# Attention scores: bias and maximum in one VectorE instruction, one score matmul, and the head split moved to ScalarE and GpSimd

## The reference, cut to what matters

```python
s_loc = jnp.einsum('bjqhd,bkjchd->bhjqkc', qb, k_slab, preferred_element_type=F32) * NA_SCALE
s_loc = jnp.where(mask6, s_loc + bias[None], -jnp.inf)
s_ctx = jnp.einsum('bjqhd,bmhd->bhjqm', qb, kc, preferred_element_type=F32) * NA_SCALE
s = jnp.concatenate([s_loc.reshape(B, H, n_cb, NB_COLS, n_loc), s_ctx], axis=-1)
p = jax.nn.softmax(s, axis=-1).astype(v.dtype)
o = (jnp.einsum('bhjqkc,bkjchd->bjqhd', p_loc, v_slab)
     + jnp.einsum('bhjqm,bmhd->bjqhd', p[..., n_loc:], vc))
```

## Time and profile before

| | us |
|---|---|
| median of 3 runs | 2961.95 |
| lowest and highest of the runs | 2944.74 and 2966.42 |
| the profiled execution's own time | 2960.28 |
| its span | 2958.5 |
| TensorE busy | 2811.8 (95%) |
| VectorE, ScalarE, GpSimd busy | 1488.5, 767.6, 884.8 |
| mean granted TensorE clock | 0.961 of full |

### The profile page before, as it was taken

One profiled execution on the slowest core, in us unless ns is written; L12 is line 12 of the kernel. 1 busy time (PEld: TensorE's weight loads), 2 busy tenths in 40 slices (PEclk: granted clock), 3 DMA queues, 4 the chain that ended last, 5 costly groups with the idle time before them and its releaser, 6 DMA issues.

```text
span 2958.5 us, 40428 instructions
## 1 busy us (share of the span) xinstructions
PE 2811.8 (95%) x15289; PEld 2625.9 (89%) x15289; DVE 1488.5 (50%) x2513; ACT 767.6 (26%) x1035; POOL 884.8 (30%) x355
## 2 busy tenths in 40 slices
PE   6899999999999989999999999999998887899998
PEld 6799999998965889999999899999997775778887
DVE  6666455655324265554665622422327888432233
ACT  1322111112134232211112322111114666332222
POOL 0232223322311122232333222322323443344442
PEclk6899999999969999999999999999999998999999
DMA  5244334432300023433444122312211111233332
GB/s 194 85 113 122 99 113 122 134 85 75 107 5 19 27 77 110 130 108 111 118 116 117 51 64 83 102 56 64 74 54 44 53 53 50 65 96 100 89 104 80
DMA packets 413083, 256.78 MB, mean 87 GB/s; under 512 B 6653, under 2 KB 405846, under 8 KB 413014
## 3 DMA queue, kind: packets, MB, share of 16 engines
q1 hardware_dynamic: 413014, 255.87, 29.9%
HBM read 252.70 MB, written 4.25 MB: 87 GB/s over the span
## 4 chain that ended last, share of the span: by engine, by line
PE 64%; issue 20%; DVE 7%; POOL 5%; ACT 3%; DMA 0%; SPq 0%; POOLq 0%; DVEq 0%; ACTq 0%
PE pair_b L1536 28%; PE pair_a L1536 27%; POOL w_lo L641 5%; PE pair_c L1586 2%; DVE decay L1496 1%; PE pair_c L1817 1%; DVE ada_sums L1015 1%; DVE decay L1494 1%; DVE h_lo L1154 1%; PE pair_b L1792 1%; DVE gate_i L1490 1%; PE pair_a L1776 1%; PE pair_a L1777 1%; PE pair_a L1778 1%; PE pair_a L1526 1%
## 5 line engine op out<-in xcount | busy, mean ns | idle before, releaser
L641 POOL TENSOR_TENSOR w_lo<-raw,w_hi 128x1024 fp32r<-128x1024 f32 (+3 forms) x302 | 825.4, 2734 | 1843.7 <-ACT w_hi L733 1843.7
L733 ACT ACTIVATE w_hi<-raw 128x1024 fp32r<-128x1024 f32 (+3 forms) x302 | 337.2, 1117 | 1284.9 <-PE pair_b L1536 438.8
L1045 DVE TENSOR_TENSOR work_g<-work_s,pair_b 128x768 f32<-128x768 f32 (+1 forms) x88 | 78.1, 888 | 698.7 <-PE pair_b L1536 535.9
L1015 DVE SCALAR_TENSOR_TENSOR ada_sums<-ada_raw,cvec,ada_sums 128x256 f32<-128x256 f32 x896 | 395.6, 514 | 0.0
L1536 PE MATMUL pair_a<-h_hi,w_hi 128*128 128x384 f32 x1312 | 340.7, 340 | 12.6 <-POOL w_lo L641 9.6
L1536 PE MATMUL pair_a<-h_lo,w_hi 128*128 128x384 f32 x1312 | 335.7, 337 | 0.0
L1536 PE MATMUL pair_a<-h_hi,w_lo 128*128 128x384 f32 x1312 | 335.6, 337 | 0.0
L1536 PE MATMUL pair_b<-h_hi,w_hi 128*128 128x384 f32 x1168 | 296.9, 335 | 3.8 <-POOL w_lo L641 3.8
L1536 PE MATMUL pair_b<-h_hi,w_lo 128*128 128x384 f32 x1168 | 296.7, 334 | 0.0
L1536 PE MATMUL pair_b<-h_lo,w_hi 128*128 128x384 f32 x1168 | 296.6, 334 | 0.0
L1536 PEld LDWEIGHTS pair_a<-h_hi,w_hi 128*128 128x128 f32 x1312 | 236.2, 190 | 16.7 <-issue 12.6
(11 more groups left out here) (273 smaller groups left out, 4602.6 us busy)
## 6 DMA issues: line engine op xcount, KB each, us to landing
raw<-in_ffn_w_gu_dram SPq DMA_DIRECT2D x176, 512.0 KB, 4.0
ada_raw<-in_ada_w_dram SPq DMA_DIRECT2D x64, 1024.0 KB, 5.2
raw<-in_ffn_w_down_dram SPq DMA_DIRECT2D x64, 704.0 KB, 5.3
raw<-in_rg_w_in_dram SPq DMA_DIRECT2D x20, 512.0 KB, 3.8
ada_first<-in_ada_w_dram SPq DMA_DIRECT2D x4, 2048.0 KB, 17.6
raw<-in_ab_w_in_dram SPq DMA_DIRECT2D x16, 512.0 KB, 3.9
raw<-in_rg_w_out_dram SPq DMA_DIRECT2D x8, 640.0 KB, 4.4
raw<-in_ab_w_out_dram SPq DMA_DIRECT2D x8, 512.0 KB, 4.1
```

The source lines that it names most:

```text
L641: nc.gpsimd.tensor_tensor(wl[:, par, 0:kt * P], raw[:, par, 0:kt * P], wh[:, par, 0:kt * P].bitcast(F32), ALU.subtract).then_inc(split_rea ...
L733: nc.scalar.activation(wh[:, par, 0:kt * P], raw[:, par, 0:kt * P], ACT.Copy).then_inc(hi_done, 1)
L1015: step = nc.vector.scalar_tensor_tensor(out=sums[v], in0=tiles(k), scalar=c_k, in1=sums[v], op0=ALU.mult, op1=ALU.add)
L1045: nc.vector.tensor_tensor(gbuf[:, 0, 0:W], sbuf[:, 0, 0:W], up, ALU.mult)\
```

## The change

It computes the same result with the work laid out in another way.

- Queries are scaled by a negative factor, and mask and bias are built with opposite sign, so that the scores in PSUM are negated. A latent step's scores are one product of 512 columns, whose keys are two runs of 256 columns in `k_t`. The product of identity and bias is gone.
- One DVE instruction, `tensor_tensor_reduce`, reads the 512 negated scores from PSUM and the bias (a run of 256 columns of bias, then 256 zeros) from SBUF, writes their sum to `prob` in SBUF and the minimum of each row to `neg_max`. It takes the place of `reduce_max`.
- ACT's exponential reads `prob` in SBUF, in place, with scale -1. `prob` has three buffers, the row statistics four.
- `scores(s)` waits for the new DVE instruction of `s - 2` and no longer for the exponential. The wait for a head's bias moves from PE to DVE, POOL's wait for a free bias buffer moves from the score matmul to the new DVE instruction.
- `take_heads` on DVE keeps the two copies. The high part is made by ACT (`heads_high`, at `j` = 5 of heads 2, 4, 6, and after the loop) and the low part by POOL (`heads_low`, after the bias of heads 3, 5, 7, and after the loop).
- PE starts the output projection when the four pooling tiles are split, and waits for each head tile where it is first read. `values` of a new pair of heads waits for the copies alone.
- `prob` moves to the place of `p_t`, `prob_t` and the bias table to other free places.

```diff
+            def heads_low(t):
+
+                pool.wait_ge(heads_hi, t + 1)
+                nc.gpsimd.tensor_tensor(hl[:, KP + t, :], att_f[:, t % 2, :], hh[:, KP + t, :].bitcast(F32),
+                                        ALU.subtract).then_inc(mixed_split, 1)
...
-                    pool.wait_ge(scores_done, (BLOCKS + 2) * (h - 2) + BLOCKS)
+                    pool.wait_ge(max_done, (BLOCKS + 2) * (h - 2) + BLOCKS)
                 for v in range(3):
                     t = bass.AP(tensor=table[:, :, :].tensor, offset=table[:, h % 2, SHIFT[v]:SHIFT[v] + 1].offset,
                                 ap=[list(table[:, 0, 0:1].ap[0]), [1, SLAB], [RPB_C, GRID_R]])
-                    last = nc.gpsimd.tensor_tensor(bias[:, h % 2, v, :].rearrange("p (c r) -> p c r", r=GRID_R), t,
-                                                   mask[:, v, :].rearrange("p (c r) -> p c r", r=GRID_R), ALU.add)
+                    last = nc.gpsimd.tensor_tensor(bias[:, h % 2 * 3 + v, :].rearrange("p (c r) -> p c r", r=GRID_R),
+                                                   mask[:, v, :].rearrange("p (c r) -> p c r", r=GRID_R), t, ALU.subtract)
                 last.then_inc(bias_done, 1)
+                if h in (3, 5, 7):
+                    heads_low(h // 2 - 1)
+            heads_low(KP - 1)
...
+            def heads_high(t):
+
+                act.wait_ge(heads_taken, t + 1)
+                nc.scalar.activation(hh[:, KP + t, :], att_f[:, t % 2, :], ACT.Copy).then_inc(heads_hi, 1)
+
             for s, (h, j) in enumerate(STEPS):
                 W = NK + CTX if j < BLOCKS else CTX
-                b = s % 2
 
                 act.wait_ge(max_done, s + 1)
-                if s >= 2:
-                    act.wait_ge(turned_done, s - 1)
-                nc.scalar.activation(prob[:, b, 0:W], pA[:, b * 512:b * 512 + W], ACT.Exp, bias=rowmax[:, b:b + 1],
-                                     accum_out=rowsum[:, b:b + 1]).then_inc(prob_done, 1)
+                nc.scalar.activation(prob[:, s % 3, 0:W], prob[:, s % 3, 0:W], ACT.Exp, bias=rowmax[:, s % 4:s % 4 + 1],
+                                     scale=-1.0, accum_out=rowsum[:, s % 4:s % 4 + 1]).then_inc(prob_done, 1)
                 if s >= 1:
                     copy_turned(s - 1)
+                if j == 5 and h % 2 == 0 and h >= 2:
+                    heads_high(h // 2 - 1)
             copy_turned(len(STEPS) - 1)
+            heads_high(KP - 1)
...
-                    dst, scale = (kT, 1.0) if n == 2 else (qT, DH ** -0.5)
+                    dst, scale = (kT, 1.0) if n == 2 else (qT, -DH ** -0.5)
...
-            def normalise(s):
+            def lowest(s):
+
                 h, j = STEPS[s]
                 W = NK + CTX if j < BLOCKS else CTX
                 b = s % 2
+                if j == 0:
+                    dve.wait_ge(bias_done, h + 1)
+                if s >= 3:
+
+                    dve.wait_ge(turned_done, s - 2)
+                add = bias[:, 6, :]
+                if j < BLOCKS:
+
+                    n = h % 2 * 3 + VARIANT[j]
+                    add = bass.AP(tensor=bias[:, :, :].tensor, offset=bias[:, n, 0:1].offset,
+                                  ap=[list(bias[:, 0, 0:1].ap[0]), [(6 - n) * NK, 2], [1, NK]])
+                src, to = pA[:, b * 512:b * 512 + W], prob[:, s % 3, 0:W]
+                if j < BLOCKS:
+                    src, to = [a.rearrange("p (g n) -> p g n", n=NK) for a in (src, to)]
+                dve.wait_ge(scores_done, s + 1)
+                nc.vector.tensor_tensor_reduce(out=to, in0=src, in1=add, scale=1.0, scalar=3.0e38, op0=ALU.add, op1=ALU.min,
+                                               accum_out=rowmax[:, s % 4:s % 4 + 1]).then_inc(max_done, 1)
+
+            def normalise(s):
+
+                j = STEPS[s][1]
+                W = NK + CTX if j < BLOCKS else CTX
                 dve.wait_ge(prob_done, s + 1)
-                chain(nc.vector.reciprocal(rowinv[:, b:b + 1], rowsum[:, b:b + 1]))
-                nc.vector.tensor_scalar(prob[:, b, 0:W], prob[:, b, 0:W], rowinv[:, b:b + 1], None, ALU.mult)\
-                    .then_inc(prob_scaled, 1)
+                nc.vector.reciprocal(rowinv[:, s % 4:s % 4 + 1], rowsum[:, s % 4:s % 4 + 1]).then_inc(inv_done, 1)
+                dve.wait_ge(inv_done, s + 1)
+                nc.vector.tensor_scalar(prob[:, s % 3, 0:W], prob[:, s % 3, 0:W], rowinv[:, s % 4:s % 4 + 1], None, ALU.mult)                    .then_inc(prob_scaled, 1)
 
             def take_heads(t):
 
                 dve.wait_ge(pv_done, (2 * t + 2) * (BLOCKS + 2))
+
+                dve.wait_ge(mixed_split, KP + t - 1)
                 f = att_f[:, t % 2, :]
                 o, oc = pC[:, (t % 2) * 512:(t % 2) * 512 + SEQ], pR[:, (t % 2) * 512:(t % 2) * 512 + CTX]
                 nc.vector.tensor_copy(f[:, 0:SEQ].rearrange("p (r c) -> p r c", c=GRID_W),
                                       o[:, ::-1].rearrange("p (c r) -> p r c", r=GRID_R))
-                chain(nc.vector.tensor_copy(f[:, SEQ:T], oc))
-                chain(nc.vector.tensor_copy(hh[:, KP + t, :], f))
-                nc.vector.tensor_tensor(hl[:, KP + t, :], f, hh[:, KP + t, :].bitcast(F32), ALU.subtract)\
-                    .then_inc(mixed_split, 1)
+                nc.vector.tensor_copy(f[:, SEQ:T], oc).then_inc(heads_taken, 1)
 
             for s, (h, j) in enumerate(STEPS):
-                W = NK + CTX if j < BLOCKS else CTX
-                b = s % 2
-
-                dve.wait_ge(scores_done, s + 1)
-                nc.vector.reduce_max(rowmax[:, b:b + 1], pA[:, b * 512:b * 512 + W], AX_X, negate=True)\
-                    .then_inc(max_done, 1)
+                lowest(s)
                 if s >= 1:
                     normalise(s - 1)
                 if j == 3 and h % 2 == 0 and h >= 2:
                     take_heads(h // 2 - 1)
             normalise(len(STEPS) - 1)
-            take_heads(3)
+            take_heads(KP - 1)
...
-                    pe.wait_ge(prob_done, s - 1)
+                    pe.wait_ge(max_done, s - 1)
                 else:
                     pe.wait_ge(proj_done, 2 + 16)
                 bank = pA[:, b * 512:(b + 1) * 512]
                 if j < BLOCKS:
                     q = qT[rows, t, (BLOCKS - 1 - j) * P:(BLOCKS - j) * P]
-                    if j == 0:
-                        pe.wait_ge(bias_done, h + 1)
                     k0 = SLAB_AT[j] * GRID_R
-                    nc.tensor.matmul(bank[:, 0:NK], q, kT[rows, t, k0:k0 + NK], start=True, stop=False)
-                    nc.tensor.matmul(bank[:, 0:NK], ident[:, :], bias[:, h % 2, VARIANT[j], :], start=False, stop=True)
-                    last = nc.tensor.matmul(bank[:, NK:NK + CTX], q, kT[rows, t, SEQ:T], start=True, stop=True)
+                    keys = bass.AP(tensor=kT[:, :, :].tensor, offset=kT[rows, t, k0:k0 + 1].offset,
+                                   ap=[list(kT[rows, t, 0:1].ap[0]), [SEQ - k0, 2], [1, NK]])
+                    last = nc.tensor.matmul(bank[:, :].rearrange("p (g n) -> p g n", n=NK), q, keys, start=True, stop=True)
...
-                    pe.wait_ge(mixed_split, KP + t - 1)
+                    pe.wait_ge(heads_taken, t - 1)
...
-            pe.wait_ge(mixed_split, 2 * KP)
-            outputs("about", P_ABOUT, KD, hh, hl)
+            pe.wait_ge(mixed_split, KP)
+            outputs("about", P_ABOUT, KD, hh, hl, 0, lambda k: k >= KP and pe.wait_ge(mixed_split, k + 1))
```

More of the change, by code:

```diff
@@ L228, in trunk @@
         kT = att("k_t", [P, KP, T])
+        pool_at = g_at + 2 * size([P, T // P, KP * P]) + size([P, SLABS, KP * P]) + size([P, KP, T])
         pT = att("p_t", [P, KP, PADW])
+        assert pool_at == g_at + size([P, T // P, KP * P]) + size([P, SLABS, KP * P]) + 2 * size([P, KP, T])
+        late = alias(pool_at, g_end)
+        prob = late("prob", [P, 3, 512])
         att_f = at("mixed", [P, 2, T], F32, g_at)
@@ L232, in trunk @@
         v_rows = gbuf[:, 1, :]
-        prob = at("prob", [P, 2, 512], F32, scr_at)
-        prob_t = at("prob_t", [P, 2, 512], F32, scr_at + size([P, 2, 512]))
+        prob_t = at("prob_t", [P, 2, 512], F32, scr_at)
         att2 = alias(scr_at + size([P, 4, T]), SBUF_END)
-        bias = att2("bias", [P, 2, 3, NK])
-        table = att2("rpb_table", [P, 2, TABLE])
+        bias = att2("bias", [P, 2 * 3 + 1, NK])
+        table = at("rpb_table", [P, 2, TABLE], F32, scr_at + size([P, 2, PADW]))
         mask = att2("mask", [P, 3, NK])
-        rowmax = att2("neg_max", [P, 2])
-        rowsum = att2("row_sum", [P, 2])
-        rowinv = att2("row_inv", [P, 2])
+        rowmax = att2("neg_max", [P, 4])
+        rowsum = att2("row_sum", [P, 4])
+        rowinv = att2("row_inv", [P, 4])
         inv_n = att2("inv_n", [P, NB])
@@ L337, in trunk @@
         prob_done = sem("prob_done")
+        inv_done = sem("inv_done")
         prob_scaled = sem("prob_scaled")
+        heads_taken = sem("heads_taken")
+        heads_hi = sem("heads_hi")
         turned_done = sem("turned_done")
```

(11 more changed lines are left out.)

## The result

The changed kernel takes 2910.44 us (median of 4 runs, 2909.76 to 2915.29), the kernel before 2954.39 (median of 4, 2944.74 to 2966.42) beside it. The ratio is 0.9853, with a 95% interval of 0.9807 to 0.9898: 1.0 to 1.9% faster. The forecast was 2926, with a range of 2898 to 2948. The profiled execution took 2915.29 us, 45.0 less than that of before.

A forecast was written before the change was run, and what follows sets the result against it. TensorE was taken to bound the attention. Gains of 25.3 (score products), 0.7 (start), 2.1 (head split), 3.0 (hole) and 3.0 (half clock behind it) sum to 34.1 us, from 2960.3 to 2926 us, range 2898 to 2948.

The forecast's parts named there:

- Products: Attention: one score product of 512 columns at 1.04 us replaces three totalling 1.89, per latent step at 2.4 GHz.
- Start, waits and hole: TensorE gains 0.7 us at the third score, 2.1 at three head-split waits, 3.0 ahead of the output projection.
- The half clock behind the hole: Output projection's first 5.94 us at half clock should go with the hole before it: 3.0 us gained.
- I take the same time, 51.1 us: Attention's start: the low clock stretch keeps its length in time, so 4.0 us of the gain are given back.
- the early clock rival: Attention's start: about 5 us at half clock in place of 51, 21 us more off, 2905 us; chance 0.17.
- the low stretch's length is far from 51 us: Sign at the attention's start by which the forecast is wrong; about 51 us at half clock was expected.
- POOL beside DVE: Head split's low part on POOL: runs beside DVE's scaling of `prob` without delay, cost nothing in the sum.
- No wait of TensorE for DVE in the loop: Expected sign in the profile after: TensorE never waits for DVE in the attention loop.
- The cover of the loop: Loop through DVE and ACT: TensorE has 3.8 us of other work against some 3.2 needed, so cost 0.
- The bound at which DVE itself would limit the loop: Attention loop: DVE becomes the bound only if its new instruction takes above 1.9 us per latent step.
- The end: Output projection starts at once, removing TensorE's 2.96 us standstill: 3.0 us gained; last head tile ready in time.
- The weights' overhead: Score products keep 0.18 us per change of stationary operand, so the wide one costs 1.04 us and not 0.86.

The follow-up runs named there:

- experiment 9: Changed kernel with three score products of 256 columns in place of the one of 512: 2932.06 us (11 runs), ratio 0.9932 to the kernel before.
- experiment 1: Changed kernel with the head split back on DVE and TensorE waiting for all eight head tiles: 2925.16 us (10 runs), ratio 0.9932 to before.
- experiment 2: Kernel before with only the head split moved to ACT and POOL and TensorE's late waits: 2939.6 us (10 runs), ratio 0.999.
- experiment 5: Changed kernel with TensorE waiting for all eight head tiles before the output projection: 2915.72 us (4 runs), ratio 0.9876 to before.
- experiment 6: Changed kernel with the new DVE instruction issued twice for each step: 2925.29 us (8 runs), ratio 0.9911 to before.
- experiment 7: Changed kernel with the heads' low part made by DVE in place of POOL: 2912.92 us (4 runs), ratio 0.9867 to before.
- experiment 8: Changed kernel run again, unaltered: 2912.99 us (4 runs), ratio 0.9866 to before.
- experiment 4: Changed kernel with idle products in TensorE's gap at the start, three behind the second score product, one behind the third: 2907.91 us (4 runs), ratio 0.9869.
- experiment 11: Changed kernel with idle products in TensorE's gap at the start, repeated with more runs: 2906.41 us (5 runs), ratio 0.9839 to before.
- experiment 3: Kernel before with two idle products in TensorE's gap ahead of the third score product: 2938.09 us (10 runs), ratio 0.9975.
- experiment 10: Changed kernel with the split on DVE, waiting for all eight tiles, idle products in all TensorE gaps: 2917.57 us (5 runs), ratio 0.9876.

## Why the prediction was right and where it was not

**The sum for TensorE held.** The four stretches without half clock put it together: 149.25 (before, filled), 142.86 (three narrow products), 126.81 (split on DVE, filled), 119.78 (changed, filled). The prediction's terms at full clock are 30 latent steps of 0.85, 0.7, 2.1 and 3.0, together 31.3; 149.25 - 119.78 = 29.5 was measured, or 30.0 without the 0.4 and 0.9 us that the idle products cost. Products 24.0 against 25.5: the steps inside the heads gave 0.825 each (17.09 - 13.79 for four), two waits of TensorE for the scaling, 0.2 us each, are new, and of the third step's 0.85 only 0.3 came off, because its transposes wait for the softmax's start (11.49 us behind the first pooling product, against 11.80 in experiment 9). Start, waits and hole together 6.0 (149.25 - 0.4 - 142.86) against 5.8; the start alone gave 0.8 (10.73 - 9.92) against 0.7. The half clock behind the hole, 3.0 us, is gone.

**The step that failed is "I take the same time, 51.1 us".** The low stretch at the start was 10.2 us in the profile after, and 10.2 to 13.7 in experiments 1, 2, 5, 6, 7 and 8. The 40.9 us less at half clock are 18.4 us, and 2926 - 18.4 = 2907.6 is what the early clock rival said (2905, with 5 us). That rival, at 0.17, described the profile better than the forecast did: the measured 2910 lies outside the 2918 to 2934 that had 0.50, and "the low stretch's length is far from 51 us" was one of the two signs by which the forecast was to be wrong. The wide range, 2898 to 2948, holds the result because it took the rival in. The profile of before was an execution of its upper group; against the lower group, 2944, the changed kernel at 2911 gains 33 us, near the forecast's 34. So the size of the gain was right and the base was not: 2944.74 stood among the three runs, and the text used it for a rival and not for the base. That two of the four runs of before in the comparison fell into each group, so that its median lies between them, is luck.

**The clock is not mere luck either.** The kernel before falls into its upper group in 21 of 55 runs. The changed kernel has no such group in 8 runs, nor have experiments 4, 5, 7 and 11, which differ from it in small things, in 17. Long stretches stood behind a gap in the profiles of before and of experiment 1. Four of ten runs of experiment 2 and one of eleven of experiment 9 lie 16 to 32 us above the median of their others, at a lower mean clock, which fits more half clock at a place that is not on record. Where the gaps were filled (3, 4, 10, 11) no profile has a stretch of half clock inside the attention, and none of the 24 runs stands apart. What makes a stretch last 13.7 us in one run and 51.2 in another, behind the same gap of 1.42 us and the same work (experiment 2 and before), stays open, and so does why the changed kernel's stay at 10 to 14. The shape of the first steps plays a part (experiment 9), but no run separates it from the position in time.

**POOL beside DVE: wrong, and cheap.** The prediction read one overlap in which the scaling took 0.49 us and put the contention at nothing. In the changed kernel, POOL's and DVE's timelines:

```profile
879.76 1.81 POOL L676 TENSOR_TENSOR h_lo<-mixed,h_hi 128x768 fp32r<-128x768 f32 x1 [18.70 <-ACT h_hi L911]
881.52 2.67 POOL L692 TENSOR_TENSOR bias<-mask,rpb_table 128x256 f32<-128x256 f32 x3
886.02 2.77 POOL L692 TENSOR_TENSOR bias<-mask,rpb_table 128x256 f32<-128x256 f32 x3 [1.83 <-DVE neg_max L1439]
```
```profile
881.56 1.10 DVE L1449 TENSOR_SCALAR prob<-prob,row_inv 128x512 f32<-128x512 f32 x1
...
883.55 0.92 DVE L1449 TENSOR_SCALAR prob<-prob,row_inv 128x512 f32<-128x512 f32 x1
...
885.97 0.49 DVE L1449 TENSOR_SCALAR prob<-prob,row_inv 128x512 f32<-128x512 f32 x1
...
887.93 1.15 DVE L1449 TENSOR_SCALAR prob<-prob,row_inv 128x512 f32<-128x512 f32 x1
```

The same instruction takes 0.49, 0.92, 1.10 or 1.15 us. A row of POOL above merges up to three instructions of 0.85 us each. What decides is where the scaling begins inside a single one of them, and which of the two came first.

At 885.97 the scaling begins 0.06 us ahead of POOL's instruction and keeps its 0.49; that instruction then takes 1.14. At 881.56 it begins 0.04 us behind one and takes 1.10. At 883.55 it begins 0.22 us into one and takes 0.92; in experiment 6, 0.52 us in, 0.62. At 887.93 it begins at the seam of the second and the third, and takes 1.15. In each slowed case, in all the profiles, it ends as if it had waited until 0.65 to 0.68 us after the POOL instruction's start and then taken 0.49. In the earlier trace rows it began 0.66 us into a POOL instruction, where by this nothing is left to wait for. All eight scalings that overlap POOL in the trace of before began 0.66 to 0.82 us into one, so none could show the cost. (POOL's instruction there adds and has its operands in the other order; no run puts a scaling earlier into one of that form.)

The Trainium skill, "GPSIMD Engine Reference", section "1. Specifications", which has the two contend over SBUF, fits these rows, and the prediction's reading of the earlier trace rows does not. Seven scalings of 32 were slowed. On TensorE it shows in two waits:

```profile
882.71 0.42 PEld L1829 LDWEIGHTS pair_b<-ident,prob 128*128 128x128 f32 x4 [0.94 <-DVE prob L1449]
884.93 0.42 PEld L1829 LDWEIGHTS pair_b<-ident,prob 128*128 128x128 f32 x4 [0.76 <-DVE prob L1449]
```

0.76 is what every such load shows behind a wide product; 0.94 is 0.18 more, and there is one other like it. "No wait of TensorE for DVE in the loop" was wrong by 0.4 us.

**The cover of the loop held.** It was 0.6 us at 0.75 us for the DVE instruction and gone at 1.4; experiment 6 had about 1.5 and lost 0.7 us for each head in the mean. The bound at which DVE itself would limit the loop has no working in the prediction; by its own terms it is 2.65 - 0.15 - 0.49 = 2.0 us and not 1.9. Nothing hung on it, at 0.77.

**The end held.** The projection starts at 949.20, directly behind the last value products. POOL's low part takes 1.82 us where the bound was 2.7.

**The weights' overhead.** The rule of hidden weight loads (the Trainium skill, "TensorE: Matmul & The Clock Gate", section "Step-by-step: what each phase is for") would have given 0.86 us for the wide product. 1.05 was measured, near the 1.04 that the rows of before gave.

## What to carry to other kernels

Before a forecast rests on a profiled execution, see whether its time belongs to the main group of the runs; a long stretch at half clock in it is a term of its own, and it may be absent in most runs. A gap of 1 to 3 us in TensorE's work can cost far more than itself, so price a wait with the half clock that may follow it, and consider idle products to bridge it; where they are longer than the gap they cost time too. An overlap without contention in a trace shows that offset alone, and eight of them may all have the same offset; look at where each instruction begins inside the other before moving work to POOL beside DVE.

## What the runs showed of the hardware that was not expected

- Behind gaps of 1.2 to 3 us inside the attention TensorE's clock was held at 1.2 GHz for 10.2 us (changed kernel, experiments 1, 5, 6, 7), 13.7 (2, 6, 8), 44.4 (1) or 51.2 (before), while TensorE was busy but for 0.3 us at most. The length of the gap does not give the length of the stretch: 1.42 us stood ahead of 51.2 and of 13.7, 2.28 ahead of 10.2 and of 13.7, and behind two gaps of 1.2 us in experiment 6 the clock stayed up. With the gaps filled, it stayed at 2.4 GHz through the attention, 120 to 148 us of the same work (experiments 3, 4, 10, 11).
- Behind the hole at the end, where wide products of the split operands follow, half clock lasted 6.8 us (before, experiments 1 and 3) or 3.4 (5).
- A scaling of 512 columns on DVE and a POOL instruction with two SBUF inputs of 256 columns get in each other's way, and the one that begins first goes first. The scaling takes 0.49 us alone and up to 1.16 when it begins with the POOL instruction; the later it begins the less it loses, and from 0.66 us into the 0.85 it loses nothing. The POOL instruction takes 0.85 us alone and 1.05 to 1.15 behind a scaling.
- The custom DVE instruction, with one input from PSUM and one from SBUF and a minimum taken on the way, takes 691 ns for 512 columns, as long as the plain reduction it replaces, plus 83 ns to read the minimum out.
